# Gate units on two banks with 512-column products, and residual sums of mixing and cross attention made by VectorE alone

## The reference

```
p = rms_norm(h) @ w_in                       # q, k, v, g_ret, c_in, gates
y_a = (silu(g_ret) * head_group_norm(chunk_retention(q, k, v))) @ w_ret_out
c   = causal_dwconv(a * sigmoid(b), conv_dw_w, conv_dw_b)      # 31 taps; a, b from c_in
y_b = silu(layer_norm(c)) @ w_conv_out + b_conv_out
g_a, g_b = split(sigmoid(gates + b_gate), 2)                   # gates: 2048 wide
h = h + (g_a * y_a + g_b * y_b) @ w_mix_out                    # "mixing"
h = h + memory_cross_attention(rms_norm(h), mem_n) @ w_xo      # "cross"
h = h + conv_ffn(rms_norm(h), ...)
```

## Time and profile before

| | |
|---|---|
| runs | 2065.37, 2065.54, 2066.22 us, median 2065.54 |
| the profiled execution | 2065.54 us, its span 2063.8 us |
| granted TensorE clock, mean | 0.999 of full speed |
| PE busy | 2051.4 us (99% of the span) |
| PEld busy | 1962.1 us (95%) |
| DVE (VectorE) busy | 1669.2 us (81%) |
| ACT (ScalarE) busy | 1072.4 us (52%) |
| POOL (GpSimd) busy | 248.6 us (12%) |
| DMA | 361.82 MB, mean 175 GB/s |
| gates of the first mixer | 984 to 1030 us |
| gates of the second mixer | 1620 to 1666 us |

### The profile page before, as it was taken

The page is one execution under the profiler, slowest core; times in us unless marked ns, Lnnn a source line. Parts: engine busy times, 40 slices in busy tenths (PEclk is TensorE's granted clock), DMA queues, the critical chain, the costliest instruction groups (busy, mean ns, idle before and its releaser), DMA issues.

```text
span 2063.8 us, 36745 instructions
## 1 busy us (share of the span) xinstructions
PE 2051.4 (99%) x15426; PEld 1962.1 (95%) x15426; DVE 1669.2 (81%) x2461; ACT 1072.4 (52%) x1320; POOL 248.6 (12%) x175
## 2 busy tenths in 40 slices
PE   9999999999999999999999999999999999999998
PEld 9999999899999989979989999999988999989997
DVE  8988897888789788898995668677798996749775
ACT  6886344457754435355455454445346545545442
POOL 0212065000006500002101001100000300000110
PEclk9999999999999999999999999999999999999999
DMA  7663555553245465544555445456544555534543
GB/s 266 197 199 137 184 184 179 189 205 144 103 148 183 158 214 195 183 161 155 195 184 183 162 150 179 177 169 209 182 178 147 187 186 182 182 135 174 183 165 119
DMA packets 58292, 361.82 MB, mean 175 GB/s; under 512 B 6736, under 2 KB 9360, under 8 KB 21136
## 3 DMA queue, kind: packets, MB, share of 16 engines
q1 hardware_dynamic: 58128, 359.48, 49.5%
HBM read 358.37 MB, written 1.08 MB: 174 GB/s over the span
## 4 chain that ended last, share of the span: by engine, by line
PE 94%; DVE 3%; ACT 1%; issue 1%; DMA 0%; POOL 0%; SPq 0%; DVEq 0%; ACTq 0%
PE acc L638 66%; PE acc L647 11%; PE acc L637 7%; DVE w_lo L1198 1%; PE acc L769 1%; PE acc L767 1%; PE acc L768 1%; DVE arena L1386 1%; PE acc L973 1%; DVE x L1373 1%; PE pA L1022 1%; DVE in_both L1379 0%; PE pC L815 0%; PE pB L1046 0%; PE pD L1133 0%
## 5 line engine op out<-in xcount | busy, mean ns | idle before, releaser
L638 PE MATMUL acc<-in_both,w_hi 128*128 128x256 f32 x7408 | 1346.1, 284 | 3.1 <-DVE in_both L1403 1.8
L638 PEld LDWEIGHTS acc<-in_both,w_hi 128*128 128x128 f32 x7408 | 1156.2, 192 | 8.3 <-issue 3.3
L638 PE MATMUL acc<-in_both,w_lo 128*128 128x256 f32 x4656 | 1146.7, 283 | 0.1
L1198 DVE TENSOR_TENSOR w_lo<-raw,w_hi 128x2048 fp32r<-128x2048 f32 (+1 forms) x349 | 756.6, 2171 | 130.9 <-ACT w_hi L2105 130.7
L638 PEld LDWEIGHTS acc<-in_both,w_lo 128*128 128x128 f32 x4656 | 830.7, 192 | 5.0 <-POOL in_both L2734 0.4
L2105 ACT CAST w_hi<-raw 128x2048 fp32r<-128x2048 f32 (+1 forms) x349 | 630.1, 1807 | 239.4 <-PE acc L638 142.6
L2734 POOL TENSOR_TENSOR in_both<-arena,in_both 128x256 fp32r<-128x256 f32 (+1 forms) x112 | 119.7, 1069 | 1208.7 <-ACT in_both L2586 508.2
L647 PE MATMUL acc<-in_both,w_hi 128*128 128x512 f32 x952 | 227.9, 391 | 0.0
L647 PEld LDWEIGHTS acc<-in_both,w_hi 128*128 128x128 f32 x952 | 175.4, 188 | 34.2
L1886 DVE SCALAR_TENSOR_TENSOR arena<-arena,cols 128x256 f32<-128x256 f32 x480 | 200.5, 489 | 0.0
L2744 POOL TENSOR_TENSOR arena<-arena 128x256 f32<-128x256 f32 x44 | 96.2, 2187 | 375.9 <-ACT arena L2407 375.9
(11 more groups left out here) (294 smaller groups left out, 1531.7 us busy)
## 6 DMA issues: line engine op xcount, KB each, us to landing
raw<-in_wide SPq DMA_DIRECT2D x285, 1024.0 KB, 4.8
raw<-in_narrow SPq DMA_DIRECT2D x64, 704.0 KB, 4.0
arena<-cs_rows SPq DMA_DIRECT2D x16, 256.0 KB, 4.7
arena<-in_mem SPq DMA_DIRECT2D x3, 1024.0 KB, 6.9
x<-in_x SPq DMA_DIRECT2D x4, 256.0 KB, 6.2
raw<-in_wide SPq DMA_DIRECT2D x2, 512.0 KB, 5.5
tables<-in_tables SPq DMA_DIRECT2D x1, 1024.0 KB, 16.7
arena<-cs_rows SPq DMA_DIRECT2D x16, 64.0 KB, 5.2
```

What stands on the lines that cost most here:

```text
L638: return mm(outs[m], w[:, k, at], moving[:, c, :], start=start, stop=stop)
L1198: tt(w_lo[g % RAW][:, 0:n], raw[g % RAW][:, 0:n], w_hi[g % HI][:, 0:n], ALU.subtract).then_inc(lo_ready, 1)
```

## The change

In `gates`, units 0 to 6 of 8 are made side by side, each of their two tiles in a bank of its own: 16 products of 512 columns and 16 of 256. A unit holds two of the four banks, so TensorE waits until unit u - 2 is read. ScalarE copies the second halves to `gate`, VectorE adds the first halves to them and frees the banks, and ScalarE then takes the sigmoid in SBUF. Unit 7 stays as it was, but for its wait. For mix and mem_o the residual sums go to VectorE's general `residual`: per unit split(u + 2), the two adds, two high parts, two low parts, the sum of squares; in the last unit the split comes after the low parts. ScalarE keeps the casts and the squares. att_o keeps the written-out order.

```diff
+        GATES_TWO = 7
+        def gate_banks(seg, u):
+            pair = (seg.base - 1) % 4 // 2 ^ 1 ^ u % 2
+            return acc[2 * pair], acc[2 * pair + 1]
...
+                    elif seg.name == "gates" or seg.name == "ret_out" and j == 0:
+                        pe.wait_ge(acc_free, g - 1)
+                    elif seg.name == "ret_out" and j == 1:
+                        pe.wait_ge(acc_free, g - 2)
...
+                    if seg.name == "gates" and j < GATES_TWO:
+                        banks = gate_banks(seg, j)
+                        def both_inputs(m, ks):
+                            for k in ks:
+                                ins = mm(banks[m][:], hi[:, k, m * P:(m + 1) * P], in_both[:, (seg.chunk0 + k) % IN_CHUNKS].rearrange("p a l -> p (a l)"),
+                                         start=k == 0, stop=k == nk - 1)
+                            return ins
+                        for m in range(2):
+                            both_inputs(m, range(1))
+                        for m in range(2):
+                            for k in range(nk):
+                                mm(banks[m][:, 0:T], lo[:, k, m * P:(m + 1) * P], in_hi[:, (seg.chunk0 + k) % IN_CHUNKS, :], start=False, stop=False)
+                        for m in range(2):
+                            last = both_inputs(m, range(1, nk))
-                    if side_by_side(seg.name, j, seg.units):
+                    elif side_by_side(seg.name, j, seg.units):
...
@@ VectorE, residual @@
+                    else:
+                        for m in range(2):
+                            c = x[:, bass.ds(u * 2 + m, 1), :]
+                            ins = tt(c, banks[m].unsqueeze(1), c, ALU.add)
+                            E.mark(ins) if m == 0 else ins.then_inc(acc_free, 1)
...
+                    if kind == "feat" and nth is not None:
+                        E.settle()
+                        dve.wait_ge(acc_free, u + (seg_base + 1))
+                        early_parts(u * 2, 2)
...
+                    if kind == "feat":
+                        E.wait(square_a)
+                        for m in range(2):
+                            dve.wait_ge(sum_ready, u * 2 + (sums + 1 + m))
+                            tt(ssum, ssum, sq2[:, m, :], ALU.add).then_inc(sum_ready, 1)
...
@@ VectorE, mixer @@
-                    project("gates", None, last_gated)
+                    seg = take("gates")
+                    for u in range(seg.units):
+                        split(u + 2, seg, u + 2)
+                        for m in range(2 if u < GATES_TWO else 0):
+                            dve.wait_ge(side_g, 2 * (GATES_TWO * l + u) + m + 1)
+                            y = gate[:, 2 * u + m, :]
+                            ins = tt(y, y, gate_banks(seg, u)[m][:, 0:T], ALU.add)
+                            E.mark(ins) if m == 0 else ins.then_inc(acc_free, 1)
+                        last_gated(u, u, None)
...
-                    residual_pairs("mix", 4 + 3 * l, f"x_norm{l}", XN_AT)
+                    residual("mix", 4 + 3 * l, f"x_norm{l}", XN_AT)
...
-                    residual_pairs("mem_o", 5 + 3 * l, f"f_norm{l}", LATE_AT)
+                    residual("mem_o", 5 + 3 * l, f"f_norm{l}", LATE_AT)
...
@@ ScalarE @@
+            def residual_tiles(name, nth):
+                seg_base = take.base()
+                def squares(u, j, banks):
+                    act.wait_ge(acc_free, seg_base + u + 1)
+                    act.wait_ge(sum_ready, (1 + DC) * nth + 2 * u + 1)
+                    fn(sq2, x[:, 2 * u:2 * u + 2, :], ACT.Square).then_inc(square_a, 1)
+                project(name, squares)
...
+                    for u in range(seg.units):
+                        y = [gate[:, 2 * u + m, :] for m in range(2)]
+                        bias = [wcol(f"b_gate{l}", 2 * u + m) for m in range(2)]
+                        split(u + 2, seg, u + 2)
+                        act.wait_ge(unit_done, seg.base + u + 1)
+                        if u < GATES_TWO:
+                            for m in range(2):
+                                copy(y[m], gate_banks(seg, u)[m][:, T:2 * T]).then_inc(side_g, 1)
+                            act.wait_ge(acc_free, seg.base + u + 1)
+                            for m in range(2):
+                                E.mark(fn(y[m], y[m], ACT.Sigmoid, bias=bias[m]))
+                        else:
+                            banks = banks_of(seg.base + u)
+                            E.mark(fn(y[0], banks[0], ACT.Sigmoid, bias=bias[0]))
+                            fn(y[1], banks[1], ACT.Sigmoid, bias=bias[1]).then_inc(acc_free, 1)
+                        if u < 2:
+                            ret_high(l, 6 + u)
```

More of the change, by code:

```diff
@@ L403, in build @@
         side_a = sem("side_a")
+        side_g = sem("side_g")
         gated_v = sem("gated_v")
@@ L1270, in residual @@
             def residual(name, nth=None, gain=None, at=0, twice=False, beside=None, final=False):
-                kind = {"ssm_out": "deep", "down": "pair"}[name]
+                kind = {"ssm_out": "deep", "down": "pair"}.get(name, "feat")
                 seg_base, sums = take.base(), E.seen.get(sum_ready, 0)
@@ L1336, in first_and_last @@
                     first(u, j, banks)
-                    if isinstance(u, int) and u == last:
+                    if kind == "feat" and nth is not None:
+                        E.settle()
+                        dve.wait_ge(acc_free, u + (seg_base + 1))
+                        early_parts(u * 2, 2)
+                    if kind != "feat" and isinstance(u, int) and u == last:
                         sums_of(u, j)
@@ L1342, in second @@
                         beside(u, j, banks)
-                    if not (isinstance(u, int) and u == last):
+                    if kind == "feat":
[3 more added lines that the diff above has]
+                            tt(ssum, ssum, sq2[:, m, :], ALU.add).then_inc(sum_ready, 1)
+                    elif not (isinstance(u, int) and u == last):
                         sums_of(u, j)
@@ L1354, in sums_of @@
                         add_squares(u, j, u, 1)
-                marks = {"pair": 1 if twice or final else 0.5, "deep": 1}[kind]
+                marks = {"pair": 1 if twice or final else 0.5, "deep": 1, "feat": 2}[kind]
                 seg = project(name, first_and_last, second, steps={v_order: marks}, last_first=True)
@@ L2648, in run @@
                     project("conv_out", mixed, steps={val_ready: 1})
-                    residual("mix", 4 + 3 * l, f"x_norm{l}", XN_AT)
+                    residual_tiles("mix", 4 + 3 * l)
                 return run
@@ L2705, in run @@
                     x_high(l, 3)
-                    residual("mem_o", 5 + 3 * l, f"f_norm{l}", LATE_AT)
+                    residual_tiles("mem_o", 5 + 3 * l)
                 return run
```

## The result

The changed kernel takes **2068.76 us** (median of 20 runs, 2067.87 to 2069.88), the kernel before 2066.03 us beside it. One of the 20 runs of the kernel before took 2838.49 us; the ratio leaves it out, and without it the median is 2065.98 us. The ratio is 1.0014, 95% interval 1.0007 to 1.0020: 2.7 us slower, within the 0.2% that counts as no change, and 0.4 us from the forecast. The profiled execution took 2069.18 us.

A forecast was written before the change was run, and what follows sets the result against it. TensorE was taken as the bound, with VectorE nearly without room beside it in the gates. Gates +5.4 us and residual sums -2.5 us gave +2.9 us on 2065.54 us: 2068.4 us, range 2065 to 2071.3.

The forecast's parts named there:

- The sum: Whole kernel: gates +5.4 us, residual sums -2.5 us, together +2.9 us, giving 2068.4 us.
- part 4: Residual sums of mix and mem_o: TensorE's wait of 0.63 us at each of four places goes, -2.5 us in all.
- Part 1: Gates, TensorE alone: the wide products gain 0.19 us a unit, 2.7 us for both mixers.
- Part 2, the adds: Gates, VectorE: adds of 0.67 us a unit make its step 6.04 us, which paces TensorE once slack is used.
- Part 2, GpSimd: Gates: two GpSimd pieces asked for during taps cost VectorE 1.04 us each, 0.78 us more than before.
- The start of ret_out: After the gates: ret_out starts at 1032.65 instead of 1030.13, the gates losing 2.5 us a mixer.
- The 0.2 us in ret_out: In ret_out, VectorE without a lead needs 16.9 us against TensorE's 16.7, 0.2 us more.
- Part 3: Gates, ScalarE: chain from adds to cast, 2.75 us, stays hidden behind a 3.17 us tap; same rate from either memory.
- (a): Gates: VectorE doesn't bind, so the wide products' gain stands; -5.2 us, 2060.3 us, chance 0.06.
- (d): Gates: TensorE's gaps drop its clock to 1.2 GHz, one unit a mixer; 2080 us, chance 0.01.
- (c): Gates: GpSimd's pieces slip under the adds, 2.08 us less a mixer; -1.3 us, 2064.2 us, chance 0.08.
- (b): Last unit of mix and mem_o: VectorE comes late, the 2.5 us gain is lost; 2070.9 us, chance 0.18 with shorter-overlap adds.

The follow-up runs named there:

- e3: Changed kernel without VectorE's two adds in the seven gate units, so part of the result is missing: 2061.54 us, ratio 0.9978 to the kernel before.
- e4: Changed kernel with one more VectorE add from PSUM in gate units 1 to 6 of each mixer: 2071.41 us, ratio 1.0028 to the kernel before.
- e10: Changed kernel with only gate units 0, 1 and 2 on two banks: 2066.11 us, ratio 1.0001 to the kernel before.
- e5: Changed kernel with ScalarE's ret_high of gate units 0 and 1 moved ahead of its wait for VectorE's adds: 2066.07 us, ratio 1.0001 to the kernel before.
- e8: Kernel before with split(3) ahead of add(1) in mix and mem_o only: 2063.49 us, ratio 0.9989.
- e2: Kernel before with the change's residual sums alone, gates as before: 2063.96 us, ratio 0.9990.
- e6: Kernel before with split(3) ahead of add(1) in att_o, mix and mem_o: 2065.10 us, ratio 0.9996.

## Why the prediction was right, point by point

- **The sum.** +2.9 forecast, +2.7 measured, but that it is so close is in part luck. By stretches the change costs 2.3 us, and two errors half cancel in it: the gates lose 1.2 us less over both mixers than forecast, and part 4 wins 0.6 us less.
- **Part 1** (0.19 us a unit from the wide products): right. e3 wins 1.34 us a mixer, seven units by 0.19. The estimate of 0.04 us a unit from the Trainium skill's page "TensorE: Matmul & The Clock Gate", section "Wait — 56ns, not 53.3ns?", would have been 0.3 us; the measured number decides, since the 256-column products of this kernel start 0.12 us apart.
- **Part 2, the adds** (0.67 us a unit, none hidden once the slack is used, TensorE at VectorE's 6.04 us): right. The rows show 0.66 and 6.03; e3 takes them away and the loss goes, e4 adds to them and the time follows one to one, but for 0.28 us a mixer that GpSimd's first piece then costs less. The single waits were forecast as 0.4 to 0.5 us each; the profile shows one of 1.40 and then 0.22 each.
- **Part 2, GpSimd** (both pieces get in during a tap, 1.04 us each, 0.78 more than before): the term that was mis-sized. It is 1.43 in all, 0.13 more than before. The step that failed was that a piece asked for in the midst of a tap gets in at the next gap between two instructions. The second one did (1002.04) and cost 1.05 us, as forecast. The first did not (995.22): it stood until VectorE's adds, which read PSUM, ran in part beside them and cost 0.38. Why the two differ is open; e4 and e10 repeat both. That a piece costs less beside instructions that read PSUM is shown by e5 and e4. The rule of the Trainium skill's page "SBUF — State Buffer", section "Who interferes with whom", names the two parties rightly. The 1.30 that I worked out from it for each piece did not come out: the piece that got into a tap cost 1.05, and the other one's cost hung on who got the port next.
- **The start of ret_out** (2.5 us later a mixer): 1.89 by stretches, less by 0.63, and GpSimd's term alone is 0.65 smaller. **The 0.2 us in ret_out**: right, 0.19. VectorE's third split there ends at 1048.99, 17.0 us after the adds of unit 6; 16.9 was worked out.
- **Part 3** (ScalarE's chain stays hidden): right, and from the end of the adds to that of the cast it takes 2.74 us (1013.99 to 1016.73), where 2.75 was forecast. But the rate is not the same from either memory: two sigmoids and what follows them start 0.82 us apart from SBUF (1026.09 to 1026.91) and 0.72 from PSUM (1034.74 to 1035.46). No wait of VectorE for a cast stands in the gates, and a table load stands once, at 990.27 under the wait for the first adds, as one did before.
- **Part 4** (0.63 us at each of four places): the mechanism was right, the size 0.48. VectorE is ready 1.45 us before the last unit (1.3 forecast). But the high part of chunk 6 starts 0.86 us after the adds, against 0.78 in the earlier trace rows, and that makes it late by 0.03 us, with the small gaps behind it: 0.15 us remain. What I left unseen is that the same could be had by an order of two lines (e8).
- **Rivals.** (a) did not come. (d) did not come: with waits of up to 1.40 us the granted clock of the gates stayed at 1.00, the 2.4 GHz level. (c), both pieces slipping under the adds, did not come in the changed kernel; e5 brings most of it, 2066.07 us, with 0.39 us a mixer still paid. (b) did not come: 0.15 us is left at up_b, and the sign set for it was over 0.3.

Over both mixers the sum by stretches is +3.8 in A, +0.4 in B, -1.9 in C and D.

## What to carry to other kernels

Where a second engine is as busy as the one that bounds, as VectorE was for all 46 us here, a saving of 0.19 us a unit on the first that puts 0.67 us on the second is a loss; the same edit wins where the second engine has a lead, so put it in the units where the lead is largest and stop when it is used up. Read the lead from the timeline: how long before its use each split ends. When an engine comes late to a short critical piece, look first at what it did while it stood idle ahead of that: here, moving one instruction into the idle time won as much as a new division of labour (e8 against e2). Work the order out for each place by itself: the same two lines lost 1.3 us at att_o (e6).

## What the runs showed of the hardware that was not expected

- GpSimd's [128, 512] add, 1.30 us alone, stretched to 5.77 us when asked for within a row of VectorE instructions that read SBUF alone: five more of a tap and a split of 2.28 us passed it before it ran. In the same stage another one got in within 0.3 us. Where it runs is worth a microsecond to VectorE: 1.05 us inside a tap, 0.38 behind two adds that read PSUM, 0.06 behind three (e4), nothing where adds and gating products follow the split (e5).
- Two profiled executions of nearly the same program differ by up to 1 us at the start and the end and by 0.05 us in the stretches between, so that differences of 0.2 us in a stage can be read from single profiles where the total time needs many runs.
